# Neighbourhood bias as two fp32r parts instead of one fp32 matmul per head, its loads on SyncE's queue

## The chip, the cores and the metric

The kernel runs on one core of one Trainium2 chip. The metric is the device time of one execution in microseconds (us), lower is better. Several executions are timed and the median is given.

## The reference

The program chains two blocks of two layers each, with batch 1, 256 latent tokens, 256 context tokens and width 1024. First comes a neighbourhood attention layer and a grouped-query attention layer, each with a SwiGLU part, then two more layers with convolution, pooling, spatial gating and gated feed-forward parts. The change touches the neighbourhood attention alone. There 16 heads of 64 attend from the 256 latent tokens (a grid of 4 rows of 64 columns) to all of them, and to the context. A learned bias is added to the scores of the latent keys, and keys outside a window of 16 columns get -1e30:

```python
bias = rpb[:, drow[None, :, None], dcol[:, None, :]]
s_nb = jnp.einsum('bqhd,biwhd->bhqiw', q_r, k_b).astype(jnp.float32) * scale + bias.astype(jnp.float32)[None]
s_nb = jnp.where(col_in[None, None, :, None, :], s_nb, MASK_VALUE).reshape(b, NA_HEADS, GRID_W, n_nb)
s_cx = jnp.einsum('bqhd,bshd->bhqs', q_r, kc).astype(jnp.float32) * scale
p = jax.nn.softmax(jnp.concatenate([s_nb, s_cx], axis=-1), axis=-1).astype(v.dtype)
```

The context tokens attend to the context only, without a bias. All inputs and the output are fp32.

## The kernel before

All is written out by hand for five engines: each has its own program in its own order, and semaphores join them. Nothing is scheduled by a planner.

**Weights.** The weights are cut into chunks of 1024x256, 1 MB each. SyncE (SP) loads them into one of three slots (`raw`), ScalarE copies a chunk to fp32r (`wh`, L333), and VectorE subtracts that from the fp32 chunk for the low part (`wl`, L340). TensorE multiplies with three fp32r matmuls instead of one in fp32: high by high, high by low, low by high (`three`, L356). Every matmul goes through the helper `mm`, so L354 stands for all of them in the profile. A chunk is split two chunks ahead of its use (`AHEAD`). SP's queue (`sync_program`, L284) is one list of loads: weight chunks and chunks of the modulation weights (`in_ada_w`) in turn, each waiting until its slot is free, and before the chunk `first_o0 + 5` it waits for the end of the first attention, to load seven staged chunks into room that the attention holds (L298).

**The first attention.** It runs over 8 head pairs `p`, each with four steps of 128 queries, in the order `qt` = 2, 3 (context), 0, 1 (latent). Step `i` of TensorE (`attention_pe`) is: scores of item `i`, transposes of item `i - 2` (L846), and in every other step the values of two items before. The scores (`score0`, L989) are three fp32r products of the split queries and keys (`jit`), 256 columns wide for context items and 512 for latent ones. For latent items follows the bias:

```python
            if qt < 2:
                pe.wait_ge(B.masked, 4 * p + 4)
                for h in range(2):
                    last = mm(b[h][:, 0:T], rev, bias_t[:, p % 2, h, 2 - 2 * qt:6 - 2 * qt, :].rearrange("p a b -> p (a b)"), False, True)
            last.then_inc(A0.s, 1)
```

The bias tile holds the learned table in reversed column order, and the matmul with the fixed 0/1 matrix `rev` (a part of `cst`) turns it round and adds it onto the scores in PSUM.
VectorE takes the maximum of a step (L909), ScalarE the exponential (L876), TensorE transposes, ScalarE and VectorE copy a head each back (L887, L923; of context items one of them copies both, L889, L925), and the values follow. Between these, at fixed places (`prep0`), ScalarE and VectorE split the next pair's queries and keys (L981, L986). The value results go through L896, L937, L900 and L943.

**The bias.** POOL (GpSimd) does it alone (`bias_pool`, L701), for each pair in one of two buffers of `bias_t`: four loads of 96 KB from the table with rows of 256 bytes (L709), then four masks (L714, L717). The first two pairs follow when the small loads have been transposed (`C.turned`), far ahead of the attention; pair `g` of the others when the scores of pair `g - 2` are done (`A0.s`).

Of the kernel before, what the change touches and what calls it, by code (L numbers as in the profile page):

```python
# [8 lines left out]
F32 = mybir.dt.float32  # L9
F32R = mybir.dt.float32r  # L10
ALU = mybir.AluOpType
ACT = mybir.ActivationFunctionType
AX = mybir.AxisListType

P = 128
D = 1024
KT = D // P
T = 256
# [59 lines left out]
def semaphores(nc, stage, names):  # L78

    names = names.split()  # L80
    return namedtuple(stage, names)(*[nc.alloc_semaphore(f"{stage}_{n}") for n in names])
# [12 lines left out]
def program(nc, ins, out):  # L94
    with ExitStack() as ctx:
# [4 lines left out]
        def sb(name, shape, dt=F32):  # L100
            return ctx.enter_context(nc.sbuf_tensor(name, shape, dt))
# [6 lines left out]
        adas = sb("adas", [P, 256])[:, :]  # L108
        small = sb("small", [P, 64])
        gain = sb("gain1", [P, 2])  # L110
        rq = sb("rq", [P, 32])
        rk = sb("rk", [P, 16])
        hT = sb("hT", [P, KT, TT])
# [10 lines left out]
        def at(kib, name, shape, dt=F32):  # L124
            n = int(np.prod(shape[1:])) * 4
            assert kib * 1024 + n <= arena_size, (name, kib, n)
            return nc.alloc_sbuf_tensor_at(name, shape, dt, offset=arena + int(kib * 1024))
# [5 lines left out]
        qT = at(0, "qT0", [P, KT, TT])  # L133
        kT = at(16, "kT0", [P, KT, TT])
        vtok = at(32, "vtok0", [P, 4, D])
        bias_t = at(48, "bias", [P, 2, 2, 6, 64])
        xh0, xl0 = at(62, "xh0", [P, KT, TT], F32R), at(78, "xl0", [P, KT, TT], F32R)
        vrow = at(48, "vrow", [P, 3, P])
        pre = {kib: at(kib, f"pre{kib}", [P, 1, 2048]) for kib in (0, 8, 16, 24, 32, 40, 54, 62, 70, 78, 86)}
# [35 lines left out]
        rev = cst[:, C_REV:C_REV + P]  # L175
# [108 lines left out]
        def sync_program():  # L284
            for (dst, src), landed in zip(x_loads, (L.x, L.ctx)):
                sp.e.dma_start(dst, src).then_inc(landed, 16)
            def load_staged(many):
                for a in many:
                    sp.e.dma_start(view(pre[staged[a]], 0, ada_src(a)), ada_src(a)[0]).then_inc(s_pre[lane[a][0]], 16)  # L289

            load_staged(range(3))
            for p, (kind, x) in enumerate(dma):
                if p == 1:
                    load_staged((3,))
                elif p == 2:
                    sp.wait_ge(C.vt, 1)
                    load_staged((4,))
                elif (kind, x) == ("w", first_o0 + 5):  # L298
                    sp.wait_ge(A0.pv, 16)
                    sp.wait_ge(A0.scaled, 16)  # L300
                    load_staged(range(20, 27))
                elif (kind, x) == ("w", first_ffn0 + 12):
                    sp.wait_ge(A.used, 27)
                    load_staged(range(38, 41))
                elif (kind, x) == ("w", where[st_ffn0[2][1][0]] + 4):
                    sp.wait_ge(W.used, where[st_ffn0[2][1][0]])
                    load_staged(range(34, 38))
                elif (kind, x) == ("w", first_o1 + 5):
                    sp.wait_ge(A1.s, base1.s + 16)
                    sp.wait_ge(A.used, 41)  # L310
                    load_staged(range(44, 48))
                if p >= NRAW:
                    kind_before, before = dma[p - NRAW]
                    if kind_before == "ada":
                        sp.wait_ge(A.used, before + 1)
                    else:
                        sp.wait_ge(W.hi, before + 1)
                        sp.wait_ge(W.lo, before + 1)
                src = ada_src(x) if kind == "ada" else weights[x]
                sp.e.dma_start(view(raw, p % NRAW, src), src[0]).then_inc(s_raw[p % NRAW], 16)  # L320
            sp.wait_ge(FIN.yd, 2)
            sp.wait_ge(FIN.ya, 2)
            sp.e.dma_start(out.rearrange("a (t p) d -> p (a t) d", p=P), y[:, :, :]).then_inc(FIN.out, 16)
            sp.wait_ge(FIN.out, 16)
# [28 lines left out]
        def mm(o, l, r, start, stop, shared=False):  # L353
            return pe.e.matmul(o, l, r, start=start, stop=stop, skip_group_check=shared)  # L354
# [340 lines left out]

        B = semaphores(nc, "bias", "in0 in1 masked")
        rpb = ins["na_rpb"]

        def bias_pool(g):  # L701
            s = g % 2
            landed = (B.in0, B.in1)[s]
            if g >= 2:
                pool.wait_ge(A0.s, 4 * (g - 1))
            for half in range(2):
                for q in range(2):
                    src = bass.AP(rpb.tensor, (2 * g + q) * 465 + (5 - half) * 31 + 15 - 63, [[1, 64], [31, 6], [1, 64]])
                    pool.e.dma_start(bias_t[64 * half:64 * half + 64, s, q, :, :], src).then_inc(landed, 16)  # L709
            pool.wait_ge(landed, 64 * (g // 2 + 1))  # L710
            for half in range(2):
                b = bias_t[64 * half:64 * half + 64, s, :, :, :].rearrange("p a b c -> p (a b) c")
                lo, hi = b[:, :, 0:48], b[:, :, 16:64]
                pool.e.affine_select(out=lo, in_=lo, compare_op=ALU.is_ge, fill=MASK, base=-55, pattern=[[0, 12], [1, 48]],  # L714
                                     channel_multiplier=1).then_inc(B.masked, 1)
                pool.wait_ge(B.masked, 4 * g + 2 * half + 1)
                pool.e.affine_select(out=hi, in_=hi, compare_op=ALU.is_ge, fill=MASK, base=54, pattern=[[0, 12], [-1, 48]],  # L717
                                     channel_multiplier=-1).then_inc(B.masked, 1)

# [269 lines left out]
        def score0(i, b):  # L989
            p, qt = its0[i]  # L990
            pe.wait_ge(J0.lo, 2 * p + 2)
            w, c = slice(qt * P, qt * P + P), slice(0 if qt < 2 else T, TT)
            for n, (x, y) in enumerate(((0, 2), (0, 3), (1, 2))):
                for h in range(2):
                    r = slice(64 * h, 64 * h + 64)
                    last = mm(b[h][:, 0:nk0(i)], jit[r, p % 2, x, w], jit[r, p % 2, y, c], n == 0, n == 2 and qt >= 2)
            if qt < 2:
                pe.wait_ge(B.masked, 4 * p + 4)
                for h in range(2):
                    last = mm(b[h][:, 0:T], rev, bias_t[:, p % 2, h, 2 - 2 * qt:6 - 2 * qt, :].rearrange("p a b -> p (a b)"), False, True)  # L1000
            last.then_inc(A0.s, 1)

        def values0(j, c, h):
            p, qt = its0[j]
            return vtok[:, c if qt < 2 else c + 2, P * p + 64 * h:P * p + 64 * h + 64]

        def prep0(split):
            def go(i):
                if i // 4 < 7 and i % 4 in (1, 2):
                    split(i // 4 + 1, i % 4 - 1)  # L1010
            return go

        def attention0_pe():
# [4 lines left out]

        def attention0_act():
            act.wait_ge(W.used, where["qkv0", 11] + 1)  # L1020
            attention_act(C0, prep0(split_pair_hi))

        def attention0_dve():
            attention_dve(C0, prep0(split_pair_lo))

        def attention0_pool():
            for g in range(2, 8):
# [1203 lines left out]
```

## Time and profile before

| | |
|---|---|
| median of 3 runs | 1600.87 us (1599.76 to 1603.91) |
| profiled execution | 1600.98 us |
| its span | 1599.8 us |
| TensorE matmuls busy | 1560.6 us, 98% |
| VectorE, ScalarE, POOL busy | 901.0, 682.0, 88.0 us |
| granted TensorE clock, mean | 0.994 |

The span reaches from the first to the last instruction on the core; the execution's time holds some 1.2 us beside it. The first attention lies between 185 and 285 us of the span. A matmul's recorded length holds the time through the array, so that lengths overlap, and the distance of starts tells what one costs in a row. PE stands for TensorE's matmuls, PEld for its weight loads, DVE for VectorE, ACT for ScalarE, POOL for GpSimd, SPq for SyncE's DMA queue.

### The profile page before, as it was taken

The page shows a single profiled execution, that of the slowest core. Times are in us where ns is not written, and L with a number is a line of the kernel's source. Part 1 is how long each engine was busy: PE and PEld are TensorE (multiplying, and loading weights), DVE is VectorE, ACT ScalarE, POOL GpSimd, SP SyncE. Part 2 cuts the span into 40 slices and gives each one's busy share as a digit, 9 for nine tenths or more (in the row PEclk, how much of TensorE's full clock was granted, in tenths as well). Part 3 has the DMA queues.
Part 4 walks back from the last instruction along what each step waited for, and adds up shares of the span by engine and source line. Part 5 has one row for each costly group of instructions (what it writes and reads, how often), then busy time and mean ns, then how long its engine had stood idle before and what let it go on. Part 6 is the DMA issues. An engine that isn't in the chain of part 4 may idle for free.

```text
span 1599.8 us, 25708 instructions
## 1 busy us (share of the span) xinstructions
PE 1560.6 (98%) x11195; PEld 1386.1 (87%) x11195; DVE 901.0 (56%) x1176; ACT 682.0 (43%) x923; POOL 88.0 (6%) x124
## 2 busy tenths in 40 slices
PE   6999999999999999999999999999999999999998
PEld 4778866867888888878768999999999999999998
DVE  5422477463333433357866655568777656677763
ACT  4312476342212322235764444544545446555552
POOL 2210052000000000000000000034000000000000
PEclk8999999999999999999999999999999999999999
DMA  9864532745533232364134555565555554555551
GB/s 334 249 192 158 142 31 20 263 136 187 179 105 105 80 105 74 98 230 152 54 112 153 177 192 172 176 213 173 171 186 182 189 180 155 166 180 185 178 173 71
DMA packets 242976, 251.19 MB, mean 157 GB/s; under 512 B 4797, under 2 KB 240672, under 8 KB 242864
## 3 DMA queue, kind: packets, MB, share of 16 engines
q1 hardware_dynamic: 240080, 244.33, 46.2%
q0 software_dynamic: 2464, 5.09, 2.6%
q8 instruction: 88, 1.44, 0.4%
q14 instruction: 24, 0.20, 0.0%
q10 hardware_dynamic: 320, 0.13, 0.0%
HBM read 248.49 MB, written 1.05 MB: 156 GB/s over the span
## 4 chain that ended last, share of the span: by engine, by line
PE 88%; DVE 4%; ACT 2%; POOL 2%; issue 1%; DMA 1%; SPq 1%; DVEq 0%; ACTq 0%; POOLq 0%
PE psum L354 86%; PE psum L846 2%; DMA pre<-in_ada_w 1%; DVE sums L909 1%; POOL ptmp L1736 1%; DVE pt L923 1%; ACT wh L333 1%; DVE wl L340 1%; SPq L289 0%; DMA raw<-in_ada_w 0%; POOL ptmp L1735 0%; ACT scr L876 0%; DVE acc L1515 0%; POOL scr L1743 0%; ACT xh L624 0%
## 5 line engine op out<-in xcount | busy, mean ns | idle before, releaser
L354 PE MATMUL psum<-xh,wh 128*128 128x256 f32 (+1 forms) x1936 | 615.8, 318 | 5.0 <-DVE xl L668 2.8
L354 PE MATMUL psum<-xl,wh 128*128 128x256 f32 (+1 forms) x1936 | 609.3, 315 | 0.0
L354 PE MATMUL psum<-xh,wl 128*128 128x256 f32 (+1 forms) x1936 | 609.1, 315 | 0.0
L340 DVE TENSOR_TENSOR wl<-raw,wh 128x2048 fp32r<-128x2048 f32 (+1 forms) x186 | 419.1, 2254 | 273.1 <-ACT wh L333 272.9
L333 ACT ACTIVATE wh<-raw 128x2048 fp32r<-128x2048 f32 (+1 forms) x186 | 348.2, 1874 | 389.8 <-PE psum L354 385.0
L354 PEld LDWEIGHTS psum<-xh,wh 128*128 128x128 f32 x1936 | 370.2, 191 | 37.8 <-issue 10.0
L354 PEld LDWEIGHTS psum<-xh,wl 128*128 128x128 f32 x1936 | 370.2, 191 | 22.6
L354 PEld LDWEIGHTS psum<-xl,wh 128*128 128x128 f32 x1936 | 370.4, 191 | 21.9 <-issue 0.7
L354 PE MATMUL psum<-ah,wh 128*128 128x256 f32 (+1 forms) x704 | 217.9, 310 | 0.0
L354 PE MATMUL psum<-ah,wl 128*128 128x256 f32 (+1 forms) x704 | 217.9, 310 | 0.0
L354 PE MATMUL psum<-al,wh 128*128 128x256 f32 (+1 forms) x704 | 217.9, 310 | 0.0
L354 PEld LDWEIGHTS psum<-al,wh 128*128 128x128 f32 x704 | 134.4, 191 | 6.9
L354 PEld LDWEIGHTS psum<-ah,wl 128*128 128x128 f32 x704 | 134.4, 191 | 6.9
L354 PEld LDWEIGHTS psum<-ah,wh 128*128 128x128 f32 x704 | 134.4, 191 | 6.8
L1072 DVE SCALAR_TENSOR_TENSOR hT<-psum,mod,hT 128x256 f32<-128x256 f32 x64 | 26.6, 477 | 82.8 <-PE psum L354 82.8
L909 DVE TENSOR_REDUCE sums<-psum 128x1 f32<-128x512 f32 (+1 forms) x96 | 53.0, 594 | 30.0 <-PE psum L354 29.5
L354 PE MATMUL psum<-wh,xh 128*128 128x256 f32 x224 | 65.0, 290 | 0.0
L354 PE MATMUL psum<-wl,xh 128*128 128x256 f32 x224 | 63.3, 283 | 0.0
L354 PE MATMUL psum<-wh,xl 128*128 128x256 f32 x224 | 63.3, 283 | 0.0
L1190 DVE SCALAR_TENSOR_TENSOR scr<-scr,psum 128x512 f32<-128x512 f32 x22 | 14.1, 683 | 82.8 <-ACT scr L1152 82.8
L1152 ACT ACTIVATE scr<-psum 128x512 f32<-128x512 f32 x22 | 11.9, 595 | 100.0 <-PE psum L354 100.0
L846 PE MATMUL psum<-cst,scr 128*128 128x128 f32 x320 | 44.1, 277 | 8.3 <-DVE pt L923 7.2
(254 smaller groups left out, 1568.2 us busy)
## 6 DMA issues: line engine op xcount, KB each, us to landing
raw<-in_ffn_w_in SPq DMA_DIRECT2D x44, 1024.0 KB, 4.9
raw<-in_ada_w SPq DMA_DIRECT2D x25, 1024.0 KB, 5.3
pre<-in_ada_w SPq DMA_DIRECT2D x23, 1024.0 KB, 9.9
raw<-in_w_ffn_gate SPq DMA_DIRECT2D x22, 1024.0 KB, 5.2
raw<-in_w_ffn_up SPq DMA_DIRECT2D x22, 1024.0 KB, 5.2
raw<-in_ffn_w_out SPq DMA_DIRECT2D x16, 1024.0 KB, 5.0
raw<-in_w_ffn_down SPq DMA_DIRECT2D x16, 1024.0 KB, 5.0
raw<-in_na_w_qkv SPq DMA_DIRECT2D x12, 1024.0 KB, 5.6
```

The lines of the kernel that those rows point to most:

```text
L333: act.e.activation(wh[:, c % NSPL, 0:z], raw[:, p % NRAW, 0:z], ACT.Copy).then_inc(W.hi, 1)
L340: dve.e.tensor_tensor(wl[:, c % NSPL, 0:z], raw[:, p % NRAW, 0:z], wh[:, c % NSPL, 0:z].bitcast(F32), ALU.subtract).then_inc(W.lo, 1)
L354: return pe.e.matmul(o, l, r, start=start, stop=stop, skip_group_check=shared)
L846: last = pe.e.transpose(bank[4 + h][:, c * P:(c + 1) * P], scr[:, 2 * (j % 3) + h, c * P:(c + 1) * P], ident)
L909: dve.e.tensor_reduce(m, bank[2 * (i % 2) + h][:, 0:A_.nk(i)], AX.X, ALU.max, negate=True).then_inc(S.max if A_.rms is None else S.raw, 1)
L923: dve.e.tensor_copy(A_.pt[:, g % 2, 1, :, q], bank[5][:, :].rearrange("p (c q) -> p c q", q=P)).then_inc(S.copied_d, 1)
L1072: dve.e.scalar_tensor_tensor(hT[:, k, w], b[m][:, w], mod_col(l, j, k, s), hT[:, k, w], ALU.mult, ALU.add).then_inc(O0.res, 1)
L1152: act.e.activation(scr[:, (2 * p + m) % 6, :], a[m][:, :], ACT.Tanh, scale=0.5).then_inc(G0.tanh, 1)
L1190: dve.e.scalar_tensor_tensor(s, s, 1.0, a[m][:, :], ALU.add, ALU.mult).then_inc(G0.g1, 1)
L1736: pool.e.tensor_tensor(dst[:, d:T], src[:, d:T], src[:, 0:T - d], ALU.add).then_inc(E.step, 1)
```

## The change

The masked bias of a pair is split like the weights: ScalarE copies all of it (128x768) to fp32r (`bias_h`), VectorE subtracts that and writes the low part in place over the bias (`bias_l` lies on `bias_t`). `rev` is copied once to fp32r (`rev_r`). The bias of a head is then two fp32r matmuls. `bias_h` lies at 88 KiB of the arena, in room that the projection's input (`xl0`) holds until the projection is done, so pair 0 is converted at the start of the attention; pair `g` is converted in step `4 g` of both engines, the first step of pair `g`, two steps before it is needed. The 32 loads move from POOL's queue to SP's: pairs 0 and 1 before weight chunk 8, pairs 2 to 7 before chunk `first_o0 + 5`, each with the wait that POOL had.

```diff
+        rev_r = sb("rev_r", [P, P], F32R)
...
-        bias_t = at(48, "bias", [P, 2, 2, 6, 64])
+        bias_t, bias_h, bias_l = (at(kib, name, [P, 2, 2, 6, 64], dt) for kib, name, dt in ((48, "bias", F32), (88, "bias_h", F32R), (48, "bias_l", F32R)))
...
+                elif (kind, x) == ("w", 8):
+                    sp.wait_ge(C.turned, 2)
+                    load_bias(0)
+                    load_bias(1)
                 elif (kind, x) == ("w", first_o0 + 5):
+                    for g in range(2, 8):
+                        sp.wait_ge(A0.s, 4 * (g - 1))
+                        load_bias(g)
...
+        def load_bias(g):
+            for half in range(2):
+                for q in range(2):
+                    src = bass.AP(rpb.tensor, (2 * g + q) * 465 + (5 - half) * 31 + 15 - 63, [[1, 64], [31, 6], [1, 64]])
+                    sp.e.dma_start(bias_t[64 * half:64 * half + 64, g % 2, q, :, :], src).then_inc((B.in0, B.in1)[g % 2], 16)
+
+        def bias_act(g):
+            b, h, _ = bias_parts(g)
+            act.wait_ge(B.masked, 4 * g + 4)
+            act.wait_ge(A0.s, 4 * (g - 1))
+            act.e.activation(h, b, ACT.Copy).then_inc(B.hi, 1)
+
+        def bias_dve(g):
+            b, h, low = bias_parts(g)
+            dve.wait_ge(B.hi, g + 1)
+            dve.e.tensor_tensor(low, b, h.bitcast(F32), ALU.subtract).then_inc(B.lo, 1)
 
         def bias_pool(g):
             s = g % 2
             landed = (B.in0, B.in1)[s]
-            if g >= 2:
-                pool.wait_ge(A0.s, 4 * (g - 1))
-            for half in range(2):
-                for q in range(2):
-                    src = bass.AP(rpb.tensor, (2 * g + q) * 465 + (5 - half) * 31 + 15 - 63, [[1, 64], [31, 6], [1, 64]])
-                    pool.e.dma_start(bias_t[64 * half:64 * half + 64, s, q, :, :], src).then_inc(landed, 16)
             pool.wait_ge(landed, 64 * (g // 2 + 1))
...
             if qt < 2:
-                pe.wait_ge(B.masked, 4 * p + 4)
+                pe.wait_ge(B.lo, p + 1)
                 for h in range(2):
-                    last = mm(b[h][:, 0:T], rev, bias_t[:, p % 2, h, 2 - 2 * qt:6 - 2 * qt, :].rearrange("p a b -> p (a b)"), False, True)
+                    for t in (bias_h, bias_l):
+                        last = mm(b[h][:, 0:T], rev_r[:, :], t[:, p % 2, h, 2 - 2 * qt:6 - 2 * qt, :].rearrange("p a b -> p (a b)"), False, t is bias_l)
...
-        def prep0(split):
+        def prep0(split, bias):
             def go(i):
                 if i // 4 < 7 and i % 4 in (1, 2):
                     split(i // 4 + 1, i % 4 - 1)
+                elif 0 < i < 32 and i % 4 == 0:
+                    bias(i // 4)
             return go
...
         def attention0_act():
             act.wait_ge(W.used, where["qkv0", 11] + 1)
-            attention_act(C0, prep0(split_pair_hi))
+            act.wait_ge(L.rest, NREST)
+            act.e.activation(rev_r[:, :], rev, ACT.Copy)
+            bias_act(0)
+            attention_act(C0, prep0(split_pair_hi, bias_act))
 
         def attention0_dve():
-            attention_dve(C0, prep0(split_pair_lo))
+            bias_dve(0)
+            attention_dve(C0, prep0(split_pair_lo, bias_dve))
```

ScalarE's order at the start of the attention. L780 (L803 in the changed kernel, whose lines have moved) copies the last piece of the projection, L876 (L899) is the exponential. Before:

```order
L780 ACTIVATE vtok_51<-psum 128x2x256 [waits w_used]
L876 ACT_TABLE_LOAD
L876 ACTIVATE scr,sums<-psum,sums 128x256 [waits att_max] x2
L981 ACTIVATE jit<-qT_49 128x512
L876 ACTIVATE scr,sums<-psum,sums 128x256 [waits att_max] x2
```

And after the change:

```order
L803 ACTIVATE vtok0_51<-psum 128x2x256 [waits w_used]
L1048 ACTIVATE rev_r<-cst 128x128 [waits load_rest]
L723 ACTIVATE bias_h_53<-bias_52 128x768 [waits bias_masked]
L899 ACT_TABLE_LOAD
L899 ACTIVATE scr,sums0<-psum,sums0 128x256 [waits att_max] x2
L1004 ACTIVATE jit_70<-qT0_49 128x512
```

The two copies stand ahead of the table load of the exponential.

VectorE's order in the first pairs after the change, from the last copy ahead of the attention (L461, before L453) on. L932 is the maximum (before L909), L946 and L948 the copies of transposed scores (before L923, L925), L1009 the split of queries and keys (before L986):

```order
L461 COPY adas<-psum 128x256
L728 TENSOR_TENSOR bias_l<-bias,bias_h 128x768
L932 TENSOR_REDUCE sums<-psum 128x1 x4
...
L932 TENSOR_REDUCE sums<-psum 128x1 x2
L946 COPY pt_71<-psum 128x4x128
L950 RECIPROCAL sums<-sums 128x2
L728 TENSOR_TENSOR bias_l<-bias,bias_h 128x768
L932 TENSOR_REDUCE sums<-psum 128x1 x2
L946 COPY pt_71<-psum 128x4x128
L950 RECIPROCAL sums<-sums 128x2
L1009 TENSOR_TENSOR jit<-qT_49,jit 128x512
```

The two rows of L728 are new; without them the order is that of before.

SP's queue around the loads of pairs 0 and 1 after the change. Before, it had the same rows without L713, and L709 on POOL had the loads:

```order
L328 DMA raw<-in_ada_w 128x8x256 [waits w_lo,w_hi]
L713 DMA bias<-in_na_rpb 64x6x64 [waits c_turned]
L713 DMA bias<-in_na_rpb 64x6x64 x7
L328 DMA raw<-in_na_w_qkv 128x8x256 [waits ada_used]
L328 DMA raw<-in_ada_w 128x8x256 [waits w_lo,w_hi]
```

Eight loads now stand ahead of weight chunk 8.

## Rows read from the trace of the kernel before

**Rows 1.** The page's head: span, and busy time by engine

```profile
span 1599.8 us, 25708 instructions
PE 1560.6 (98%) x11195; PEld 1386.1 (87%) x11195; DVE 901.0 (56%) x1176; ACT 682.0 (43%) x923; POOL 88.0 (6%) x124
```

**Rows 2.** The chain that ended last: start us, us, engine and line; 60 to 180, 198 to 234

```profile
61.51 118.55 PE psum L354 x784
...
219.31 0.70 DVE pt L923
```

**Rows 3.** Busy time of each engine in one stretch of a head pair

```profile
core 0: us, PE busy (x) PEld busy (x) DVE busy (x) ACT busy (x) POOL busy (x), PEclk, DMA share, GB/s
224.00:236.00 12.00, 11.67 (x97) 8.21 (x96) 8.80 (x21) 8.48 (x25) 5.07 (x9) 1.00 0.41 36
```

**Rows 4.** Timeline of TensorE in a latent score step: start us, us, engine, line, operation

```profile
211.74 0.81 PE L354 MATMUL psum<-bias,cst 128*128 128x256 f32 x3
212.39 0.27 PE L846 MATMUL psum<-cst,scr 128*128 128x128 f32 x1
```

**Rows 5.** Timeline of TensorE in the projection, 15 fp32r passes in a row

```profile
173.78 0.28 PE L354 MATMUL psum<-wl,xh 128*128 128x256 f32 x1
...
175.46 0.28 PE L354 MATMUL psum<-wh,xh 128*128 128x256 f32 x1
```

**Rows 6.** Groups by form: line, operation, count, busy us, mean ns; idle before

```profile
L981 ACT ACTIVATE jit<-kT 128x512 fp32r<-128x512 f32 x7 | 4.6, 658 | 0.0
L333 ACT ACTIVATE wh<-raw 128x2048 fp32r<-128x2048 f32 x10 | 19.1, 1912 | 40.3 <-PE psum L354 39.9 <-DMA raw<-in_na_w_qkv 0.4
L986 DVE TENSOR_TENSOR jit<-qT,jit 128x512 fp32r<-128x512 f32 x7 | 4.7, 674 | 0.6 <-ACT jit L981 0.6
L340 DVE TENSOR_TENSOR wl<-raw,wh 128x2048 fp32r<-128x2048 f32 x10 | 23.8, 2377 | 27.1 <-ACT wh L333 27.1
```

**Rows 7.** Timeline at the start of the attention; in brackets idle time before, and what ended it

```profile
184.55 1.28 ACT L876 ACT_TABLE_LOAD   x1
...
186.11 1.42 DVE L909 TENSOR_REDUCE sums<-psum 128x1 f32<-128x256 f32 x4 [0.72 <-PE psum L354]
186.57 0.47 ACT L876 ACTIVATE scr<-psum,sums 128x256 f32<-128x256 f32 x1 [0.74 <-DVE sums L909]
...
187.64 0.96 PE L354 MATMUL psum<-jit 64*128 64x512 f32 x6 [1.22 <-ACT scr L876]
```

**Rows 8.** Timeline of one head pair on VectorE, ScalarE and POOL

```profile
212.59 1.29 DVE L909 TENSOR_REDUCE sums<-psum 128x1 f32<-128x512 f32 x2 [1.72 <-PE psum L354]
...
216.91 0.40 DVE L943 TENSOR_TENSOR xl<-acc,xh 128x256 fp32r<-128x256 f32 x1
...
219.31 0.60 ACT L887 ACTIVATE pt<-psum 128x512 f32<-128x512 f32 x1 [2.11 <-PE psum L846]
...
222.36 0.84 POOL L714 TENSOR_SCALAR_AFFINE_SELECT bias<-bias 64x576 f32<-64x576 f32 x1 [4.53 <-DMA bias<-in_na_rpb]
222.52 0.95 DVE L943 TENSOR_TENSOR xl<-acc,xh 128x256 fp32r<-128x256 f32 x1
...
224.65 1.29 DVE L909 TENSOR_REDUCE sums<-psum 128x1 f32<-128x512 f32 x2 [1.19 <-PE psum L354]
```

**Rows 9.** Timeline of SP's queue, ScalarE and POOL, and the landing of the bias loads

```profile
90.28 0.37 SPq L320 DMA_DIRECT2D raw<-in_ada_w  x1
97.74 0.37 SPq L320 DMA_DIRECT2D raw<-in_na_w_qkv  x1
...
108.88 1.92 ACT L333 ACTIVATE wh<-raw 128x2048 fp32r<-128x2048 f32 x1 [10.19 <-PE psum L354]
...
215.25 2.58 POOL L709 DMA_DIRECT2D bias<-in_na_rpb  x4 [1.00 <-PE psum L354]
...
225.02 0.74 POOL L717 TENSOR_SCALAR_AFFINE_SELECT bias<-bias 64x576 f32<-64x576 f32 x1
...
285.64 13.79 SPq L289 DMA_DIRECT2D pre<-in_ada_w  x7
...
DMA to landing us min/median/max: 4.0/5.1/9.7
```

More of the change, by code:

```diff
@@ L694, in setup_dve, with bias_parts @@
             first_low(7)
-        B = semaphores(nc, "bias", "in0 in1 masked")
+        B = semaphores(nc, "bias", "in0 in1 masked hi lo")
         rpb = ins["na_rpb"]
+        def load_bias(g):
[3 more added lines that the diff above has]
+                    sp.e.dma_start(bias_t[64 * half:64 * half + 64, g % 2, q, :, :], src).then_inc((B.in0, B.in1)[g % 2], 16)
+        def bias_parts(g):
+            return [t[:, g % 2, :, :, :].rearrange("p a b c -> p (a b c)") for t in (bias_t, bias_h, bias_l)]
+        def bias_act(g):
[7 more added lines that the diff above has]
+            dve.e.tensor_tensor(low, b, h.bitcast(F32), ALU.subtract).then_inc(B.lo, 1)
         def bias_pool(g):
```

## The prediction, made before the changed kernel ran

> **What bounds the kernel now.** I read the page's head first, then the chain of waits around the change, then the busy time by stretches, then the timeline of one head pair. The head [rows 1] gives the span, 1599.8 us, and TensorE at 98% of it. The chain [rows 2] says where that figure is to be believed: ahead of the attention it lies on TensorE for 118.55 us without a break, so nothing that runs there beside it is worth anything. In the attention it leaves TensorE once per head pair, for the 0.70 us in which VectorE copies the transposed scores (L923). The pair repeats every 12.06 us, as the two long reductions at 212.59 and 224.65 show [rows 8], so TensorE holds the chain for some 94% of it. In a stretch of one such pair VectorE is busy 8.80 us of 12 and ScalarE 8.48 [rows 3]. The attention is thus bound by TensorE, with a VectorE that has about 3 us left, and the bias matmuls are on the bound.
>
> **The change part by part.** The executed profile took 1600.98 us, 0.1 above the median of 1600.87; the sum is made against the former.
>
> 1. The bias matmuls. Each of the 16 score steps with bias (8 pairs, two blocks each) runs four passes now, two for each head in fp32, and four after, two for each head in fp32r: the count stays, the length of a pass changes. In the timeline the second bias pass starts at 211.74 and the first transpose behind the fourth at 212.39 [rows 4]: three passes in 0.65 us, 0.217 each. A fp32r pass of the same shape (128x128 weights of its own, 256 columns) is in the projection just ahead: the starts at 173.78 and 175.46 are 14 passes apart [rows 5], 0.120 each. The first pass of a step waits for its weights in either form, which I leave alike. Four passes save 4 x 0.097 = 0.39 us, and 16 steps **6.2 us**, all on the chain.
>
> A page's figure would make this more. The Trainium skill, "TensorE: Matmul & The Clock Gate", section "Back-to-back issue gap", gives 262 cycles for 256 columns, which is 0.109 us at 2.4 GHz, and with it four passes would save 0.43 and the sixteen steps 6.9 us, an estimate from that page. The rows say 0.120, where every pass loads weights, and I keep the rows.
>
> 2. ScalarE makes the high part: 8 copies of 128x768. Its copies of 512 elements take 0.658 us and of 2048 1.912 [rows 6], which puts 768 at 0.87. For pairs 1 to 7 it stands behind the exponentials of the last block of a pair and ahead of the copy at 219.31, where ScalarE idles 2.11 us [rows 8]: hidden, with some 1.2 us to spare. Without that cover it would be 0.87 a pair.
>
> 3. VectorE makes the low part: 8 subtractions of 128x768, by 0.674 for 512 and 2.377 for 2048 elements [rows 6] 0.96 each. For pairs 1 to 7 it stands behind the copy at 219.3. What is behind it on VectorE is a nearly closed row of work up to the long reduction at 224.65, ahead of which 1.19 us are idle; a pair earlier it was 1.72 [rows 8]. The two shorter score steps bring that reduction's input 0.77 us sooner. So 1.19 - 0.96 - 0.77 = -0.5 to 1.72 - 0.96 - 0.77 = 0: the reduction starts up to half a microsecond late against TensorE's new time. TensorE does not ask for its exponentials until two steps on, after a transpose and a value product, some 2 us later, so most of this is cover. Bounds: nothing, or the whole 0.5 in each of 7 pairs, 3.5 us. I take **0.2 us** in all, near the first end, because the chain shows no wait on these exponentials in the steady pairs.
>
> 4. The start. The buffer of the high part lies in room that the projection's input holds, so the conversion of pair 0 cannot run until the projection is done. ScalarE is free at 184.55 and now loads its table there, 1.28 us, done at 185.8, in time for the first exponential at 186.57 [rows 7]. With the reversal matrix copied (128x128; nearest row the 512-element copy, less 384 elements at the slope of step 2, about 0.35) and pair 0's 0.87 ahead of it, the table is done at 187.1. VectorE subtracts from 185.8 to 186.7, so its first reduction moves from 186.11 to 186.7. The exponential starts at 187.1 instead of 186.57 and TensorE's third score step, now at 187.64, waits for it. Cost **0.5 us**; bounds 0 (the third step's wait has other slack) and 1.2 (all the added ScalarE work).
>
> 5. The loads. 32 DMAs of 96 KB leave POOL's queue for SP's. Eight stand between SP's issues at 90.28 and 97.74 [rows 9]. At 0.37 us each they are issued by 93.7, before the next one is due. If one takes 13.79 / 7 = 1.97, as the seven staged loads do, that weight chunk goes out 8 us late; it is split at 108.88, two chunks ahead of its use, and a chunk is 10.19 idle and 1.92 busy there, 12.1 us [rows 9], so that too is hidden. The other 24 stand in SP's empty wait before 285.64. Each is released by the same event as before. POOL took about 2.6 us to issue four. The last of the four masks of a pair ends at 225.8, 10.5 us after 215.25, where its loads were issued [rows 9]; ScalarE asks for it when it is through with the exponentials of the next pair's last block, 2.11 us ahead of 219.31 [rows 8] and a shortened pair of 11.3 us later: 13.2 us behind the event, 2.7 us to spare at the loads' old pace. Taken at **0** either way. POOL is relieved, but nobody waits for POOL.
>
> Sum: 6.2 - 0.2 - 0.5 = 5.5 us. 1600.98 - 5.5 = **1595.5 us**.
>
> **The rivals.** 0.3% is 4.8 us here, so the border of "faster" is 1596.1, close to the forecast.
>
> (a) VectorE begins to pace the pairs. For: of the 3 us it had left, 0.96 go to the subtraction and 0.77 to the shorter pair, and the masks now come earlier, beside its subtractions. At 222.52 one of them took 0.95 us instead of 0.40 (216.91) with a POOL mask started at 222.36 [rows 8]. One more such disturbance and the lateness of step 3 a pair, 0.4 us in 7 pairs, is 2.8: 1598.3. Against: the slack of 2 us behind that reduction.
>
> (b) On the other side: every mask blocks VectorE. A pair has four masks of 0.74 us. If each stops a VectorE subtraction for its whole length, VectorE needs 8.80 + 0.96 + 4 x 0.74 = 12.7 us a pair, without any idle time, against 12.06: six pairs lose 0.66 and the two others keep their 0.77, so 4.0 + 0.5 - 1.5 = +3.0, 1604.0. It decides as soon as the added waits pass 2.3 us a pair. Against it speaks that the masks already lie beside VectorE's work and the row that grows most grows by 0.55.
> The Trainium skill, "SBUF — State Buffer", section "Who interferes with whom", has the rule for it: a VectorE instruction with two SBUF inputs contends with a GpSimd instruction that reads SBUF, and the loser is held for the whole of the other. By that rule this change adds a candidate in each pair; the trace agrees in kind with its 0.95 against 0.40.
>
> (c) The loads land too late. If SP needs 1.97 us for each of four issues, the masks end 5.3 us later than now. Of that 2.7 and ScalarE's idle 1.2 cover 3.9; the other 1.4 stop ScalarE ahead of the copy that TensorE waits for, in six pairs: 8.4 us, 1603.9. The same follows if the landing takes 9.7 us (the longest) in place of 5.1 [rows 9].
>
> (d) The fp32r form brings nothing here, or less. It is refuted in advance by the 0.120 of [rows 5], unless the reversal matrix behaves otherwise; then only the start is left, 1601.5.
>
> (e) More than forecast: the start hidden, or passes of 0.109, up to 6.9 us: 1594.1.
>
> **How the numbers follow.** The forecast with its own bounds (4.6 to 6.2 us, 1594.8 to 1596.4): 0.60. (a) 0.27, (b) 0.03, (c) 0.04, (d) 0.02, (e) 0.04. The likeliest has 0.92 of its chance beyond 4.8 us, with (e) 0.59 in all; the rest of it, (a), (d) and the milder halves of (b) and (c) lie within 4.8; slower by more is the worse half of (b) and of (c), should both blocks and landings be at their longest. Faster 0.59, same 0.38, slower 0.03. The range goes from (e), 1594.2, to just past (a), 1598.6.
>
> **What would show it.** Bias passes 0.12 apart, and the step from the first bias pass to the first transpose 0.58 us instead of 0.97. The pair's period down from 12.06 to about 11.3. The first reduction at 186.7 and the third score step near 188.1. VectorE's idle time ahead of the long reduction gone in most pairs. SP's bias issues one behind the other, each well under 1 us, and no wait of ScalarE for a mask. It is wrong if TensorE waits in the steady pairs for an exponential or for VectorE's last-block copy (a), if masks stretch the new subtraction several times a pair (b), or if ScalarE stands ahead of its bias copy (c).

## The result, and the profile after

The changed kernel takes 1595.03 us in the median (4 runs, 1593.55 to 1596.05), the kernel before 1602.34 beside it (4 runs, 1599.76 to 1603.91): ratio 0.9951, 95% interval 0.9936 to 0.9967. Two later comparisons, on one chip at different times, gave 0.9968 (0.9959 to 0.9977) and 0.9962 (0.9949 to 0.9975). It is faster by 0.3 to 0.5%, which is 5 to 7 us as the medians fall. The profiled execution took 1595.65 us against 1600.98 of the one before. Its head, to be laid beside [rows 1]:

```profile
span 1594.3 us, 25726 instructions
...
PE 1553.4 (97%) x11195; PEld 1381.7 (87%) x11195; DVE 909.5 (57%) x1184; ACT 688.3 (43%) x932; POOL 67.3 (4%) x92
```

TensorE has as many matmuls as before and is busy 7.2 us less. VectorE and ScalarE have their 8 and 9 new instructions.

**The bias passes.** The timeline of TensorE in the same score step as [rows 4] (start us, us, engine, line, operation):

```profile
212.42 0.39 PE L362 MATMUL psum<-bias_h,rev_r 128*128 128x256 f32 x1
212.64 0.28 PE L362 MATMUL psum<-bias_l,rev_r 128*128 128x256 f32 x1
212.76 0.28 PE L362 MATMUL psum<-bias_h,rev_r 128*128 128x256 f32 x1
212.88 0.28 PE L362 MATMUL psum<-bias_l,rev_r 128*128 128x256 f32 x1
213.00 0.27 PE L869 MATMUL psum<-cst,scr 128*128 128x128 f32 x1
```

The passes start 0.12 apart, and from the first to the first transpose it is 0.58 us, where it was 0.97.

**The pair.** The chain that ended last, around this pair (start us, us, what), as in [rows 2]:

```profile
219.53 0.70 DVE pt L946
...
230.81 0.70 DVE pt L946
```

The rows of the chain that are left out between these two are TensorE's and short issue times only, as before. The pair repeats every 11.28 us instead of 12.06, 0.78 less: twice the 0.39 of a step. Beside it, the timeline of ScalarE, VectorE and POOL, which answers to [rows 8] (in brackets idle time before, and what ended it):

```profile
217.45 0.84 ACT L723 ACTIVATE bias_h<-bias 128x768 fp32r<-128x768 f32 x1
...
219.53 0.60 ACT L910 ACTIVATE pt<-psum 128x512 f32<-128x512 f32 x1 [1.23 <-PE psum L869]
...
220.21 0.94 DVE L728 TENSOR_TENSOR bias_l<-bias,bias_h 128x768 fp32r<-128x768 f32 x1
...
222.06 0.68 DVE L946 COPY pt<-psum 128x512 f32<-128x512 f32 x1
...
222.45 0.74 POOL L737 TENSOR_SCALAR_AFFINE_SELECT bias<-bias 64x576 f32<-64x576 f32 x1 [6.70 <-DMA bias<-in_na_rpb]
...
222.73 1.00 DVE L1009 TENSOR_TENSOR jit<-qT,jit 128x512 fp32r<-128x512 f32 x1
...
223.33 0.99 POOL L740 TENSOR_SCALAR_AFFINE_SELECT bias<-bias 64x576 f32<-64x576 f32 x1
...
223.65 0.95 DVE L966 TENSOR_TENSOR xl<-acc,xh 128x256 fp32r<-128x256 f32 x1
...
224.52 0.68 DVE L932 TENSOR_REDUCE sums<-psum 128x1 f32<-128x512 f32 x1
```

The high part fills most of ScalarE's idle stretch and leaves 1.23 us of it. VectorE has no idle time from its copy at 219.53 to the long reduction at 224.52; before, that reduction had 1.19 or 1.72 us idle ahead of it. Two of its subtractions here run beside masks and are stretched, 1.00 where other instances have 0.67, and 0.95 where they have 0.40. The new one is never touched: 0.94 in all seven pairs and 0.96 at the start.

**The start**, as in [rows 7]:

```profile
185.26 0.30 ACT L1048 ACTIVATE rev_r<-cst 128x128 fp32r<-128x128 f32 x1
185.46 0.83 ACT L723 ACTIVATE bias_h<-bias 128x768 fp32r<-128x768 f32 x1
...
186.27 0.98 PE L362 MATMUL psum<-jit 64*128 64x256 f32 x12 [0.55 <-DVE adas L461]
186.31 1.28 ACT L899 ACT_TABLE_LOAD   x1
186.32 0.96 DVE L728 TENSOR_TENSOR bias_l<-bias,bias_h 128x768 fp32r<-128x768 f32 x1
187.20 1.41 DVE L932 TENSOR_REDUCE sums<-psum 128x1 f32<-128x256 f32 x4
187.65 0.47 ACT L899 ACTIVATE scr<-psum,sums 128x256 f32<-128x256 f32 x1
...
188.72 1.65 PE L362 MATMUL psum<-jit 64*128 64x512 f32 x6 [1.47 <-ACT scr L899]
```

The first scores came at 186.27, 0.83 us later than in the trace before. The whole 0.83 is there already at the weight load that SP issues at 62.03 (before 61.20), ahead of anything that the change moves; so all is counted from the first score. Before, the reduction was 0.67 behind it and the third score step 2.20; now 0.93 and 2.45. The start costs 0.25 us. The table load of the exponential and the maximum that it needs are both done at 187.6, so neither alone sets this. But the row at 188.72 holds something else: six score passes took 1.65 us, not the 0.96 of [rows 7]. Busy time by stretches of 1 us (us; busy us and count of PE, PEld, DVE, ACT, POOL; granted clock; DMA share; GB/s):

```profile
188.00:189.00 1.00, 0.28 (x2) 0.28 (x4) 0.61 (x2) 1.00 (x5) 0.00 (x0) 0.80 1.10 382
189.00:190.00 1.00, 1.00 (x6) 0.56 (x6) 0.69 (x1) 1.00 (x6) 0.00 (x0) 0.50 1.03 361
...
192.00:193.00 1.00, 1.00 (x8) 0.49 (x6) 1.00 (x4) 0.70 (x2) 0.00 (x0) 0.99 0.00 0
```

For some 3.4 us, from within TensorE's wait of 1.47 us to 192, the granted clock was 0.50, the 1.2 GHz level. The trace before has 1.00 here, but a low stretch elsewhere, where the changed kernel's trace has 1.00:

```profile
1062.00:1066.00 4.00, 4.00 (x24) 4.00 (x23) 3.50 (x8) 2.10 (x2) 1.08 (x1) 0.57 0.63 211
```

**The loads** on SP's queue, as in [rows 9]:

```profile
91.14 7.24 SPq L713 DMA_DIRECT2D bias<-in_na_rpb  x8
98.57 0.60 SPq L328 DMA_DIRECT2D raw<-in_na_w_qkv  x1
...
281.95 13.73 SPq L290 DMA_DIRECT2D pre<-in_ada_w  x7
```

The eight take 0.9 us each to issue in the mean, and one of them 2.1; the median of all 32 is 0.6. The weight chunk behind the eight went out at 98.57 instead of 97.74, which is 0.83 later, as is everything there in this trace. They landed in 5.2 us in the median and 8.2 at most (before 5.1 and 9.7), and ScalarE waits for no mask.

Where the 5.5 us of the two spans went: from the first scores to SP's first staged load behind the attention (281.95, before 285.64) it is 95.68 us instead of 100.20, so 4.5 less. The later first score takes 0.8 of that away, and behind the attention another 1.8 is gained. Most of that lies around 1064, where the trace before ran at 1.2 GHz and this one did not.

### The profile page after: what moved, and what is told of

The parts are those of the page before. It is cut to its first block, busy times and chain, and to the rows that moved or that the text cites. A ratio compares the mean times of both kernels' runs of the same rounds, so it can differ in the third digit from the quotient of the medians.

```text
span 1594.3 us, 25726 instructions
## 1 busy us (share of the span) xinstructions
PE 1553.4 (97%) x11195; PEld 1381.7 (87%) x11195; DVE 909.5 (57%) x1184; ACT 688.3 (43%) x932; POOL 67.3 (4%) x92
## 4 chain that ended last, share of the span: by engine, by line
PE 88%; DVE 4%; ACT 2%; POOL 2%; issue 1%; DMA 1%; SPq 1%; DVEq 0%; ACTq 0%; POOLq 0%
PE psum L362 86%; PE psum L869 2%; DMA pre<-in_ada_w 1%; DVE sums L932 1%; POOL ptmp L1766 1%; DVE pt L946 1%; ACT wh L341 1%; DVE wl L348 1%; SPq L290 0%; DMA raw<-in_ada_w 0%; POOL ptmp L1765 0%; ACT scr L899 0%; DVE acc L1545 0%; POOL scr L1773 0%; ACT xh L632 0%
## 5 line engine op out<-in xcount | busy, mean ns | idle before, releaser
L932 DVE TENSOR_REDUCE sums<-psum 128x1 f32<-128x512 f32 (+1 forms) x96 | 52.9, 594 | 18.1 <-PE psum L362 18.0
```

Source lines behind the costliest of these rows:

```text
L932: dve.e.tensor_reduce(m, bank[2 * (i % 2) + h][:, 0:A_.nk(i)], AX.X, ALU.max, negate=True).then_inc(S.max if A_.rms is None else S.raw, 1)
```

## The experiments

Below, "the attention" is that distance, from the first scores to the first staged load behind it. The diffs are shortened: `...`, and words in place of arguments, stand for what is left out. Each ratio is against the kernel before, run beside it: 1602.32 us in the median beside the loads alone, the start alone, and the first runs with the loads on POOL and of the changed kernel again; 1603.65 beside pair 0 in fp32, the high part alone and one extra subtraction; 1602.85 beside the rest.

### The loads alone

```diff
 (kernel before; the bias stays one fp32 matmul)
+    load_bias(0), load_bias(1) ahead of weight chunk 8, load_bias(2..7) ahead of chunk first_o0 + 5
-    pool.e.dma_start(bias_t[...], src)
```

> The kernel before with only the 32 bias loads moved to SP's queue; the bias stays one fp32 matmul per head. My theory: the move is worth nothing, within 0.3% of the kernel before, the attention as long as before (185.4 to 285.6 us in that trace, 100.2 us) and the period of a head pair 12.06 us. Rival: part of the gain of the change came from relieving POOL, then this is 1 to 2 us faster. In its trace SP issues the eight early loads in 7.2 us as the changed kernel did.

Measured: 1602.65 us (12 runs), ratio 1.0 (0.9991 to 1.001); the attention 100.22 us, where it was 100.20. SP's queue in this kernel's trace:

```profile
90.45 7.36 SPq L712 DMA_DIRECT2D bias<-in_na_rpb  x8
```

The same 0.9 us each, and no weight chunk is late by it. The loads are worth nothing in either direction.

### The split with the loads left on POOL, twice

```diff
 (changed kernel)
-    load_bias(...) in sync_program
+    pool.wait_ge(A0.s, 4 * (g - 1)) and the four pool.e.dma_start, in bias_pool as before
```

> The changed kernel with the loads back on POOL's queue. My theory: the same time as the changed kernel (5 to 7 us below the kernel before), head pair period 11.29 us. Rival: the masks come later against VectorE's work and collide otherwise, which moves the period by more than 0.1 us a pair.

Measured: 1593.26 us (5 runs, 1592.89 to 1595.73), ratio 0.9952 (0.994 to 0.9964), the attention 94.19. The changed kernel, run beside it on the same chip, took 1597.39 (next section), so this kernel is 4.1 us below. It was repeated, with the changed kernel beside it once more:

> The split with the loads back on GpSimd, once more. It was 1592.9 to 1593.3 at a granted clock of 0.996 to 0.997. If that is the kernel, it is 1593.2 again and 1.3 us below the changed kernel at equal clock; if it was chance, both are at 1594.5 with the same clock. The attention takes 94.2 us where the clock does not fall.

Measured: 1595.09 us (6 runs, 1593.17 to 1597.3), the changed kernel beside it 1595.79 (8 runs, 1593.5 to 1598.93), with attentions of 94.17 and 94.19. The 4.1 us have become 0.7. The first figure came with a mean granted clock of 0.996 and 0.997 in three of its five runs; at 0.997 this kernel took 1593.0 to 1593.3 in both rounds and the changed one 1593.5 and 1593.6. With equal attentions, and nothing in the loads alone, the gain belongs to the split; a remainder of 0.2 to 0.5 us for the loads is neither shown nor excluded.

### The changed kernel again, twice

> The changed kernel once more, unedited, for a second trace and more times beside those of e1 to e3. If the longer wait at the start of the attention causes the low clock, it is there again at about 188 to 192 us; if it is chance, it is elsewhere or missing. The other low stretches (24 to 35 us, and 1062 to 1066 in the kernel before) tell how far two executions of one kernel differ by the clock alone: I expect 1 to 2 us.

Measured: 1597.39 us (11 runs, 1594.6 to 1599.14), ratio 0.9968; the attention 95.70, again with the low clock from just before 189 on. Until here the low stretch looked like a part of the change. Between executions of one kernel I had expected 1 to 2 us by the clock; these eleven lie 4.5 us apart.

> The changed kernel once more, on the same chip as the kernel with the loads back on GpSimd. If the loads on the main queue cost nothing, both have the same time within 1.5 us at equal granted clock (1594.5 at 0.996); if the loads cost something, this one is 1 us or more above the other at equal clock. The low clock at 188 to 193 us, in both traces so far, is there a third time if it belongs to this kernel, and may be absent if it is chance.

Measured: 1595.79 us (8 runs), ratio 0.9962. This time the clock stayed at 2.4 GHz. The same stretch in this trace:

```profile
188.00:192.00 4.00, 3.04 (x21) 2.06 (x22) 2.90 (x8) 3.78 (x12) 0.00 (x0) 1.00 0.62 220
```

and TensorE's timeline there:

```profile
186.51 0.97 PE L362 MATMUL psum<-jit 64*128 64x256 f32 x12 [0.55 <-DVE adas L461]
188.96 0.97 PE L362 MATMUL psum<-jit 64*128 64x512 f32 x6 [1.47 <-ACT scr L899]
...
190.96 0.73 PE L362 MATMUL psum<-jit 64*128 64x512 f32 x4
```

It is the same kernel with the same wait of 1.47 us, the third step comes again 2.45 behind the first, and its scores take 0.97 us. The attention is 94.19 us: 6.0 below before, and 1.5 below the traces with the low stretch, which is what that stretch costs.

### The conversion at the start alone

```diff
 (kernel before)
+            act.e.activation(rev_r[:, :], rev, ACT.Copy)
+            act.e.activation(bias_h[pair 0], bias_t[pair 0], ACT.Copy).then_inc(B.hi, 1)
             attention_act(C0, prep0(split_pair_hi))
...
+            dve.wait_ge(B.hi, 1)
+            dve.e.tensor_tensor(low, b, h.bitcast(F32), ALU.subtract)
             attention_dve(C0, prep0(split_pair_lo))
```

> The kernel before with only the start of the change: the reversal matrix and pair 0's bias converted by ScalarE and subtracted by VectorE ahead of the first step, their results unused, all bias matmuls fp32. It leaves nothing of the computation out. My theory of the start: the third score step comes 0.25 us later behind the first than before (2.45 instead of 2.20 us), and the granted clock then falls to 1.2 GHz for some 3 us, which costs another 1.4 us; in sum 1.7 us more attention. Rival: the low clock there is chance of one execution and not caused by the longer wait; then the trace has 0.25 us more and a clock of 1.00.

Measured: 1601.96 us (11 runs), ratio 1.0002 (0.9993 to 1.001), the attention 100.45 us. The timeline of its start:

```profile
185.72 0.98 PE L356 MATMUL psum<-jit 64*128 64x256 f32 x12 [0.55 <-DVE adas L455]
...
186.65 1.41 DVE L911 TENSOR_REDUCE sums<-psum 128x1 f32<-128x256 f32 x4
...
188.17 0.96 PE L356 MATMUL psum<-jit 64*128 64x512 f32 x6 [1.47 <-ACT scr L878]
```

Again 0.93 and 2.45 behind the first score: the start costs 0.25 us by itself, in the third step and in the attention alike. The clock stayed up, so the 1.4 us more that I expected from it did not come.

### Pair 0 left in fp32

```diff
 (changed kernel)
-            act.e.activation(rev_r[:, :], rev, ACT.Copy); bias_act(0)
-            bias_dve(0)
+            rev_r copied in bias_act(1); for p == 0: mm(b[h][:, 0:T], rev, bias_t[...], False, True)
```

> The changed kernel, but pair 0 keeps its two fp32 bias steps and nothing is converted ahead of the first step; the reversal matrix is copied together with pair 1's bias. My theory: the start is as before (third score step 2.20 us behind the first), two of sixteen steps save nothing (0.77 us lost), the 0.25 us of the start come back; with a clock of 1.00 throughout the attention takes 94.7 us against 94.2 of e2, the same within noise. Rival: the longer wait at the start makes the low clock likelier there (it was in both traces of the changed kernel and in none of the four others); then this kernel's median is about 1 us lower than that of the changed one.

Measured: 1595.62 us (5 runs, 1594.78 to 1597.88), ratio 0.9952 (0.994 to 0.9965); the attention 94.73. The start is as before the change:

```profile
186.51 0.98 PE L362 MATMUL psum<-jit 64*128 64x256 f32 x12 [0.55 <-DVE adas L461]
...
188.71 0.96 PE L362 MATMUL psum<-jit 64*128 64x512 f32 x6 [1.22 <-ACT scr L902]
```

The third step is back at 2.20. Two steps of 0.39 are given up for 0.25, so 0.5 us more than 94.19: the sum of the two terms comes out. Whether the median falls with the shorter wait, as the rival has it, is not answered: the changed kernel did not run beside this one.

### The high part alone

The matmul with the low part is left out here, so the bias has only fp32r's precision.

```diff
-                    for t in (bias_h, bias_l):
+                    for t in (bias_h,):
```

> The changed kernel without the matmul of the low part: one fp32r matmul per head instead of two (the low part is computed and left out of the scores). If TensorE still sets the period of a pair, two passes of 0.12 us less in each of 16 steps are 0.24 us a step, the pair 10.8 instead of 11.29 us and the whole 3.8 us less. Rival: VectorE, which had no idle time left ahead of its long reductions, sets it now, and the pair stays above 11.1 us.

Measured: 1592.1 us (4 runs), ratio 0.9929 (0.9916 to 0.9943). The chain:

```profile
217.87 0.70 DVE pt L946
...
228.67 0.70 DVE pt L946
```

A pair takes 10.80 us: four passes of 0.12 less, to the last hundredth. The attention is 91.82 us, with the low clock at its start: 3.9 us below the 95.70 of the changed kernel in the same condition, which is sixteen steps of 0.24. TensorE still bounds when it is given 0.48 us less work a pair, so VectorE was not at its limit at 11.28.

### More work for VectorE

In pairs 1 to 7 one subtraction of the same size as the new one is added, with a result that nothing reads, and then two.

```diff
         def bias_dve(g):
...
+            if g:
+                for _ in range(1):  # second kernel: range(2)
+                    dve.e.tensor_tensor(wl[:, 2, 768 * _:768 * _ + 768], hT[...][:, 0:768], hT[...][:, 0:768], ALU.subtract)
```

> The changed kernel with one more VectorE subtraction of 128x768 (0.94 us) in front of the existing one in each of pairs 1 to 7, its result unused. It measures what cover VectorE has left. My reading of the trace: behind the subtraction VectorE is up to 0.36 us late at one long reduction and catches up by the next context item, where it idles 0.65 to 0.84 us; so most of the 0.94 us appears: the pair goes from 11.29 to 11.4 to 12.2 us, the whole up by 1 to 6 us. Rival: the slack behind the exponentials holds it all and the pair stays at 11.29.

Measured: 1594.01 us (4 runs, 1593.35 to 1594.52), ratio 0.994 (0.9925 to 0.9955), the attention 94.18. First its timeline on VectorE, then the busy times of that pair:

```profile
217.54 0.69 DVE L949 COPY pt<-psum 128x512 f32<-128x512 f32 x1 [0.26 <-PE psum L872]
...
218.22 0.94 DVE L730 TENSOR_TENSOR wl<-hT 128x768 fp32r<-128x768 f32 x1
219.08 0.95 DVE L731 TENSOR_TENSOR bias_l<-bias,bias_h 128x768 fp32r<-128x768 f32 x1
...
223.42 1.27 DVE L935 TENSOR_REDUCE sums<-psum 128x1 f32<-128x512 f32 x2
...
228.83 0.69 DVE L949 COPY pt<-psum 128x512 f32<-128x512 f32 x1
```

```profile
217.54:228.83 11.29, 10.97 (x98) 7.82 (x98) 11.16 (x23) 9.58 (x26) 3.28 (x4) 1.00 0.30 41
```

VectorE is busy 11.16 of 11.29 us, its long reduction starts 0.9 us behind the scores, and the pair has not moved. I had expected 11.4 us or more. What I had left out is that a late reduction costs nothing until TensorE asks for the exponentials behind it.

> The changed kernel with two more 128x768 subtractions on VectorE in each of pairs 1 to 7 (0.94 us each, results unused), where one more left the pair at 11.29 us and VectorE still 0.26 us idle. If VectorE's room is what bounds now, two more make a pair longer by at least 0.94 - 0.26 - (what waits still fold away), so 11.5 to 12.0 us, and the whole by 7 x 2 x 0.2 to 0.7 = 3 to 10 us over the single-extra kernel (1597 to 1604). If TensorE alone bounds however full VectorE is, the pair stays at 11.29 us.

Measured: 1598.77 us (10 runs, 1597.46 to 1599.86), ratio 0.9978 (0.9969 to 0.9987). The chain, and the busy times of the pair:

```profile
219.81 0.69 DVE pt L949
220.50 0.07 DVE sums L953
220.57 1.73 DVE wl L730 x2
222.29 0.87 DVE bias_l L731
...
224.08 0.69 DVE pt L949
224.76 0.14 issue
224.90 0.63 PE psum L872 x4
...
231.46 0.69 DVE pt L949
```

```profile
219.81:231.46 11.65, 11.15 (x98) 7.83 (x100) 11.52 (x25) 9.58 (x27) 3.73 (x4) 1.00 0.27 35
```

Now the chain goes over VectorE for 5 us of each pair and over TensorE for the rest. The pair takes 11.65, and seven pairs make 2.5 us more than 11.29 would; the attention, with the low clock at its start, is 97.92 us, 2.2 above the changed kernel's 95.70. The place where it gives way is not the long reduction but the next copy (`pt`) behind the additions, at 224.08, for which TensorE waits. The two additions take 1.73 us of this path. Without them it needs 11.65 - 1.73 = 9.9 us a pair, 1.4 less than the 11.28 of the changed kernel. Its own trace says the same: the copy at 222.06 ends at 222.74, and TensorE's next transposes start at 224.28. That is the room on VectorE as far as this copy. Behind it, ahead of the long reduction, the kernel with one addition shows 0.9 us at least.

### TensorE kept busy in its wait

```diff
+            def keep_busy():
+                for _ in range(11):
+                    mm(bank[7][:, 0:T], jit[:, 0, 0, 0:P], jit[:, 0, 2, 0:T], True, True)
-            attention_pe(C0, score0, values0)
+            attention_pe(C0, score0, values0, keep_busy)
```

> The changed kernel with 11 more fp32r passes of 256 columns (0.12 us each, 1.3 us, their sums unused) put into the wait that TensorE has ahead of the third score step of an attention (188.72 us in the changed kernel's trace, 1.47 us idle). If the fall of the granted clock at 188 to 193 us comes from that wait, the clock stays at 2.4 GHz there, the fourth step follows the second at about 0.3 to 1.4 us less, and the attention takes 94.2 to 94.5 us instead of 95.7. If the fall comes by chance or by another cause, it is there in about as many traces as without the passes, and the attention takes 95.7 us when it is. If the passes themselves delay the scores, the third step begins later than 2.45 us behind the first.

Measured: 1595.51 us (5 runs, 1595.01 to 1596.22), ratio 0.9959 (0.9946 to 0.9972), the attention 94.17. The passes cost nothing and the clock stayed up. But it also stayed up in the changed kernel beside it on that chip, so this tells nothing of the passes.

## Why the prediction was right

The forecast was 1595.5 us and 5.5 us of gain; the median is 1595.03, and the attention, where the clock stays up, is 6.0 us shorter. That is 6.2 less the 0.25 of the start: both costs of the sum were taken too high. How near the forecast of the time came is in part luck, as the last paragraph of this section says.

**The bias passes (6.2 us).** Right in mechanism and size. A pass of 0.120, taken from the projection, is what the reversal matrix gives too. The Trainium skill, "TensorE: Matmul & The Clock Gate", section "Back-to-back issue gap", has the 262 cycles, 0.109 us, that would have made the gain 6.9, for a single matmul; of a stream with weight loads, as here, it says that both operations set the spacing. The trace agrees with the latter: three passes take 0.36, and the 6.0 us of the attention leave no room for 6.9.

**ScalarE (hidden).** Right: 0.84 for the forecast 0.87, and 1.23 us stay idle behind it.

**VectorE (0.2 us).** The subtraction measured 0.94 for 0.96, and the reduction lost its idle time. The working behind that had an error: between the copy at 219.31 and this reduction lies one of the pair's two shortened steps, not both, so its input comes 0.39 us sooner and not 0.77 (copy to reduction is 4.99 us now and was 5.34). That alone gives from 0.2 us late to 0.4 us to spare. With the masks on top, five of the seven pairs in the trace lie between 0.2 us idle and 0.2 late; the first and the last keep 1.4 us idle. It cost nothing, so the 0.2 was too much. The step's range up to 3.5 us came from a lateness of the reduction, but one more subtraction made it 0.9 us late and still cost nothing.

**The start (0.5 us).** Mechanism right, size off by half: 0.25. The reduction was forecast 1.26 us behind the first score (186.7 against 185.44) and came 0.93 behind. ScalarE begins while the copy ahead of it is still ending (185.26 in a copy that runs from 184.76 for 0.60), the reversal matrix took 0.30 for 0.35, and the starts of its two copies are 0.20 apart although the first is recorded as 0.30 long. The subtraction and the reduction behind it start 0.88 apart for 0.96. I had added up recorded durations, which overlap from one instruction to the next.

**The loads (0).** Right, and tried alone. The price of 0.37 us an issue was wrong: 0.9 in the mean of the first eight, 0.6 in the median. It lies between the two prices that the step worked with, and SP had the room for either.

**The rivals.** (a), VectorE as the pace, was given 0.27, which was too much. Its trigger came true: in four of the six pairs with masks three subtractions are stretched, by 1.0 to 1.2 us together. Two of them stand between the copy at 222.06 and the long reduction and one behind it, so what they delay is a long reduction, and the first of these could come 0.9 us late without cost. (b) asked for 2.3 us of such waits a pair, and the trace has 1.2 at most. Its rule, in the Trainium skill, "SBUF — State Buffer", section "Who interferes with whom", agrees with the rows: of VectorE's instructions beside masks only subtractions with both inputs in SBUF are stretched, and one instruction waits for the other. But (b) let each mask stop a subtraction for its whole length. In the trace the later one waits for what is left of the earlier, and where the subtraction was first, it is the mask that waits. (c) failed on its first condition, 0.6 to 0.8 us an issue in the pairs' own rows instead of 1.97. (d) fell with the passes of 0.12, and (e) had neither of its two conditions.

**What no step of it had** is the granted clock. The profiled execution, 1595.65 us, comes near the forecast because the low stretch at 188 (1.5 us) and the one at 1062 of the trace before nearly cancel, and because the first scores came 0.8 us late, which hides that the attention gained 6.0 and not 5.5. And the forecast started from 1600.98, while the kernel before had medians of 1602.3 to 1603.7 whenever it ran later: measured by medians taken together the gain is 4.9 to 7.3 us.

## What to carry to other kernels

A matmul in fp32 whose one operand is exact in fp32r (a 0/1 matrix here) cost 0.217 us per pass of 256 columns against 0.120 for the split form. So the split gained, because TensorE was the bound and the two conversions found room on other engines, and TensorE's own rows priced it. An engine that looks full for half of a stage, or for all of it (VectorE was busy 11.16 us of 11.29 with one addition), can still have room, if what it delivers late is asked for later: add work to it and see where the period moves. Before a gain of a few microseconds is explained, compare the granted clock stretch by stretch in both traces.

## What the hardware showed that I had not expected

**A VectorE subtraction and a GpSimd mask take turns, and the loss can be worked out.** The mask at 222.45 ends at 223.19. The subtraction that starts at 222.73 has 0.46 us of it ahead and grows by 0.33. The mask at 223.33 has 0.40 of that subtraction ahead and grows by 0.25, and the subtraction at 223.65 has 0.67 of that mask ahead and grows by 0.55. The same holds for all fourteen stretched subtractions and all eleven stretched masks of the attention in this trace: the one that starts second grows by what is left of the other, less 0.12 to 0.15 us. In the trace before, the 0.95 at 222.52 fits too (0.68 left, 0.55 grown). So where a mask falls decides what it costs, and the 0.94 of the new subtraction is untouched only because no mask runs beside it.

**The granted clock falls in some executions and not in others, in the same kernel.** The stretch at 0.50 at the start costs about 1.5 us (attention 95.68 and 95.70 against 94.19). The times of one kernel go with its mean clock: the changed kernel ran in 1593.5 us at a mean clock of 0.997 and in 1598.9 to 1599.1 at 0.991, the kernel before in 1599.43 at 0.996 and in up to 1605.18 at 0.992. The fastest runs of the two are 5.9 us apart, like the attentions. This spread is as large as the gain, and the three ratios of the changed kernel lie between 0.995 and 0.997.

**Whether the change makes the fall at 188 us likelier stays open.** Of nine traces in which pair 0 is split, four had it (two of three of the changed kernel, the high part alone, two extra subtractions), and five had not. Of the four traces with pair 0 in fp32, none had it. Sorted by the wait ahead of the third step instead, nine traces have it at 1.47 us, four of them with the fall, and four have it shorter (1.22 us) or filled, none with the fall. The wait of 1.47 us does not decide it alone: with the conversion at the start alone, and in the third trace of the changed kernel, it is there at full clock. Nine and four traces are too few to tell a tendency from chance, and the passes in the wait were tried once only.

**An issue on SP's queue has no fixed price.** 96 KB in rows of 256 bytes took 0.6 us in the median and up to 2.1 in the first row of eight. 1 MB of weights took 0.37 in the median, but 0.60 and 0.66 right behind those eight (98.57 and 101.93), and 1.96 each in the row of seven staged loads at 281.95. Shape and what was issued just ahead may both count; no run here separates them.
